# State-space mixer of a decoder trunk: order of PE's and SP's work around the scan, and a lag of 16 slots

## The reference, cut to what matters

```python
u = h @ in_w                                     # (256, 2048)
ug = u.reshape(Bsz, L, S5_GROUPS, S5_GROUP)      # 128 groups of 16 channels
bu = jnp.einsum('gnp,blgp->lbgn', b_bar, ug)     # 64 complex states a group
_, states = lax.associative_scan(combine, (a_seq, bu), axis=0)   # s[t] = lam * s[t-1] + bu[t]
y = jnp.real(jnp.einsum('gpn,lbgn->blgp', cmat, states)).reshape(Bsz, L, D)
y = y + d_skip.astype(f32) * u.astype(f32)
g = jax.nn.gelu(y).astype(h.dtype)
z = g @ glu_w + glu_b
val, gate = jnp.split(z, 2, axis=-1)
return val * jax.nn.sigmoid(gate)
```

## Time and profile before

| what | us |
|---|---|
| median of three runs | 2447.71 (2445.46 to 2448.32) |
| time of the profiled execution | 2444.28 |
| its span | 2442.5 |
| PE busy | 2392.6 (98%) |
| DVE busy | 1863.1 (76%) |
| ACT busy | 1039.8 (43%) |
| scan on DVE, first to last slot | 186.86 to 318.48 |
| first split product of the glu on PE | 338.03 |

### The profile page before, as it was taken

One profiled execution on the slowest core, in us unless ns is written; L12 is line 12 of the kernel. 1 busy time (PEld: TensorE's weight loads), 2 busy tenths in 40 slices (PEclk: granted clock), 3 DMA queues, 4 the chain that ended last, 5 costly groups with the idle time before them and its releaser, 6 DMA issues.

```text
span 2442.5 us, 34094 instructions
## 1 busy us (share of the span) xinstructions
PE 2392.6 (98%) x12953; PEld 1925.4 (79%) x12953; DVE 1863.1 (76%) x3012; ACT 1039.8 (43%) x1241; POOL 35.3 (1%) x68
## 2 busy tenths in 40 slices
PE   8999999999999999999999999999999999999998
PEld 5585578778888888888878888788888888888886
DVE  8469989878888887888879987887777754455457
ACT  5353134454434444344454434556444344434442
POOL 0000000000000000000000000000000000000000
PEclk9999999999999999999999999999999999999999
DMA  9978859779989997898758877646798666666674
GB/s 376 399 255 317 336 193 319 237 250 340 309 286 310 340 305 263 291 338 297 246 174 292 277 261 221 190 143 197 252 302 282 219 193 188 191 190 193 193 222 140
DMA packets 313338, 630.58 MB, mean 258 GB/s; under 512 B 26740, under 2 KB 27156, under 8 KB 313176
## 3 DMA queue, kind: packets, MB, share of 16 engines
q1 hardware_dynamic: 307664, 613.36, 74.7%
q0 software_dynamic: 4288, 13.90, 2.1%
q10 hardware_dynamic: 1224, 1.14, 0.1%
HBM read 626.20 MB, written 2.11 MB: 257 GB/s over the span
## 4 chain that ended last, share of the span: by engine, by line
PE 87%; DVE 9%; issue 2%; ACT 1%; DMA 0%; SPq 0%; DVEq 0%; ACTq 0%
PE psB L2288 39%; PE psA L2288 39%; DVE prod L1533 2%; DVE tmp L1538 1%; DVE st L1544 1%; PE psT L1838 1%; PE psM L1870 1%; DVE ada_acc L1209 1%; DVE w_lo L1192 1%; PE psB L2095 1%; PE psT L2288 0%; PE psT L1902 0%; PE psT L2083 0%; PE psA L2060 0%; PE psM L1850 0%
## 5 line engine op out<-in xcount | busy, mean ns | idle before, releaser
L1192 DVE TENSOR_TENSOR w_lo<-w_raw,w_hi 128x1024 fp32r<-128x1024 f32 x728 | 888.0, 1223 | 459.0 <-ACT w_hi L838 454.7
L838 ACT ACTIVATE w_hi<-w_raw 128x1024 fp32r<-128x1024 f32 x728 | 770.5, 1060 | 1095.0 <-PE psB L2288 476.3
L2288 PE MATMUL psB<-w_hi,hT_hi 128*128 128x512 f32 x1040 | 407.1, 391 | 0.0
L2288 PE MATMUL psB<-w_hi,hT_lo 128*128 128x512 f32 x1040 | 404.9, 389 | 0.0
L2288 PE MATMUL psB<-w_lo,hT_hi 128*128 128x512 f32 x1040 | 404.7, 389 | 0.0
L2288 PE MATMUL psA<-w_hi,hT_hi 128*128 128x512 f32 x1008 | 397.6, 394 | 2.3 <-DVE w_lo L1192 2.0
L2288 PE MATMUL psA<-w_hi,hT_lo 128*128 128x512 f32 x1008 | 392.9, 390 | 0.0
L2288 PE MATMUL psA<-w_lo,hT_hi 128*128 128x512 f32 x1008 | 392.4, 389 | 0.0
L1209 DVE SCALAR_TENSOR_TENSOR ada_acc<-ada_raw,csil,ada_acc 128x512 f32<-128x512 f32 x465 | 347.5, 747 | 14.6 <-DVE ada_acc L1209 0.5
L2288 PEld LDWEIGHTS psB<-w_hi,hT_hi 128*128 128x128 f32 x1040 | 195.2, 188 | 45.7 <-issue 4.5
L2288 PEld LDWEIGHTS psA<-w_hi,hT_hi 128*128 128x128 f32 x1008 | 189.2, 188 | 49.1 <-issue 8.0
(11 more groups left out here) (402 smaller groups left out, 2368.4 us busy)
## 6 DMA issues: line engine op xcount, KB each, us to landing
w_raw<-in_ffn_w_in SPq DMA_DIRECT2D x352, 512.0 KB, 4.6
ada_raw<-in_ada_w SPq DMA_DIRECT2D x496, 256.0 KB, 5.5
w_raw<-in_ffn_w_out SPq DMA_DIRECT2D x176, 512.0 KB, 4.6
col_raw<-in_ada_w SPq DMA_DIRECT2D x128, 512.0 KB, 7.4
w_raw<-in_dsa_in_w SPq DMA_DIRECT2D x112, 512.0 KB, 4.6
w_raw<-in_s_glu_w SPq DMA_DIRECT2D x56, 512.0 KB, 5.5
w_raw<-in_s_in_w SPq DMA_DIRECT2D x32, 512.0 KB, 7.9
w_raw<-in_dsa_out_w SPq DMA_DIRECT2D x32, 512.0 KB, 5.4
```

What stands on the lines that cost most here:

```text
L838: nc.scalar.activation(high(u), w_raw[:, u % RING], ACT.Copy).then_inc(w_hi_ready, 1)
L1192: V.tensor_tensor(low(u), w_raw[:, u % RING], high(u).bitcast(F32), ALU.subtract).then_inc(w_lo_ready, 1)
L2288: ins = MM(PS[s][:, t, 0:r.width] if into is None else into, a_[:, kt, tok], b_[:, kk, 0:r.width], start=kt == begin and m == 0, stop=kt = ...
```

## The change: a lag of 16 slots, and another order on PE and SP

`LEAD` becomes 16, so there are 143 slots, the second half follows 16 slots behind, and slot 16 waits for ACT's reads. On PE inputs 0 to 7 follow one another and the three pairs stand behind them; the four pairs with filler before outputs(0) are gone, and their units are spread further on: one pair behind outputs(0), as before, two among whole products 0 to 3 of token half 0, which now stand between outputs(0) and outputs(1), one behind outputs(1), and one in the inside part of piece 3. Of token half 1 whole products 0 to 2 stand before outputs(3), where there was only 0. On SP raw units 0 to 3 go ahead of column unit 46 (of 64), with the wait for all inputs; the others stay behind the column units.

```diff
@@ -66,6 +66,8 @@
 STATE_RING = 7
+FIRST_RAW = 4
+RAW_AT = FRONT + 46
 EARLY = 1
@@ -74,7 +76,7 @@
 HALF = CHUNKS // 2
-LEAD = 20
+LEAD = 16
@@ -699,14 +701,18 @@
                         elif m == 6:
                             sp.wait_ge(T_full, s5_in.turn + 3)
+                        if a == RAW_AT:
+                            sp.wait_ge(bu_full, 8)
+                            for k in range(FIRST_RAW):
+                                raw_unit(k)
                         col_unit(a)
-                    sp.wait_ge(bu_full, 8)
...
                         if whole(r, i, n // r.units):
-                            raw_unit(n)
+                            if n >= FIRST_RAW:
+                                raw_unit(n)
@@ -2133,8 +2139,7 @@
                     inputs(n)
-                    if 4 <= n < 7:
-                        units(2)
+                units(6)
@@ -2147,21 +2152,29 @@
                 for f in range(8):
                     outputs_inside(2, f)
                     units(2, 3)
-                for n in range(4):
-                    units(2, 3)
-                for half in range(2):
-                    pe.wait_ge(rec, rec_after(half, HALF - 1))
-                    for f in range(8 * half, 8 * half + 8):
-                        outputs(half, f)
-                        if f % 2:
-                            units(2)
-                    if half == 0:
+                pe.wait_ge(rec, rec_after(0, HALF - 1))
+                for f in range(8):
+                    outputs(0, f)
+                    if f % 2:
                         units(2)
+                units(2)
+                for k in range(FIRST_RAW):
+                    whole_products(k, 0)
+                    if k % 2 == 0:
+                        units(2)
+                pe.wait_ge(rec, rec_after(1, HALF - 1))
+                for f in range(8, KT):
+                    outputs(1, f)
+                    if f % 2:
+                        units(2)
+                units(2)
                 pe.wait_ge(gelu_done, 2)
                 for f in range(8, KT):
                     ins = outputs_inside(3, f)
+                    if f == 11:
+                        units(2)
                 ins.then_inc(inside_done, 1)
-                for k in range(glu.units):
+                for k in range(FIRST_RAW, glu.units):
                     whole_products(k, 0)
@@ -2170,11 +2183,12 @@
                 for f in range(8):
                     outputs(2, f)
                 early_products(glu.units - 1)
-                whole_products(0, 1).then_inc(w_used, 1)
+                for k in range(FIRST_RAW - 1):
+                    whole_products(k, 1).then_inc(w_used, 1)
                 pe.wait_ge(rec, rec_after(1, CHUNKS - 1))
                 for f in range(8, KT):
                     outputs(3, f)
-                for k in range(1, glu.units):
+                for k in range(FIRST_RAW - 1, glu.units):
                     if k == 4:
                         turn_row(2, M[:, 1], late_row)
                     whole_products(k, 1).then_inc(w_used, 1)
```

## The result

The changed kernel takes **2452.47 us** (median of 11 runs, 2450.73 to 2456.16), the kernel before, timed beside it, 2445.96 us (11 runs, 2444.44 to 2448.32). The ratio is **1.0027, 95% interval 1.002 to 1.0035**: the change costs 6.5 us. The forecast was no change (2447.9, range to 2451.3); the time lies above that range, close to the far end of the rival "the column stream makes PE late" (2452.9, which is +5.2 on the forecast's base of 2447.71).

What follows compares the result with a forecast made beforehand. PE was taken to bound the kernel (87% of the chain, DVE 9%), with PE and scan finishing almost together. +0.47 for outputs(2) starting later and -0.33 for a wait gone gave +0.1, 2447.9 us, range 2445.0 to 2451.3.

Steps and rivals of the forecast that it cites:

- the column stream makes PE late: Rival: units 46 and 47 land after 263.2, delaying PE at outputs(2); 2450.5 us, far end 2452.9; chance 0.15.
- Part 1: Scan on DVE, lag of 16 slots: 2.0 us less DVE work, but slot 16 needs the same 24 reads.
- part 2: Inputs in a row on PE cost nothing; DVE idles 3.6, slot 126 ends at 307.8, the scan at 319.4.
- part 3: Column units: eighth issued at about 200.6, not 190.6; units 46 and 47 land at 260.6, PE waits 3.1.
- third rival: PE's clock falls in idle stretches: 1.7 us for one fall, 3.4 for both, 2449.6 to 2451.3; chance 0.15.
- a granted clock under 1.00: Sign that the forecast is wrong: PE's granted clock below 1.00 between 190 and 320 us.
- Part 4: PE's order: 44.6 us of work, outputs(2) reached at 305.2, waits for slot 126 until 307.8; glu products at 338.2.
- The sum: +0.47 for the start of outputs(2), -0.33 for the wait gone: +0.1 us, forecast 2447.9.
- decisive threshold: The column stream decides once units 46 and 47 land after 263.2: 260.6 and the 2.6 PE has in hand.

Runs made afterwards that it cites:

- Number 1: The kernel before with a lag of 16 slots instead of 20 and nothing else: 2447.41 us against 2446.13, ratio 1.0004.
- number 3: The changed kernel with the three pairs of column units put back between inputs(4) and inputs(7), lag still 16: 2450.13 us against 2446.13 for before, ratio 1.0021.
- number 2: The kernel before with inputs 0 to 7 in a row and the three pairs behind them, nothing else: 2452.37 us against 2446.13, ratio 1.0025.
- number 8: The changed kernel with lag 20, pairs between inputs, raws before column unit 45, and PE's pairs and early products reordered: 2442.19 us against before's 2445.91, ratio 0.9985.
- number 10: The kernel of number 8 with the inputs in a row and six units behind them: 2450.12 us against 2446.35 for before, ratio 1.0019.
- number 11: The changed kernel with the lag of 20 slots again: 2453.14 us against 2446.35 for before, ratio 1.0029.
- number 9: The kernel of number 8 with the lag of 16 slots: 2448.26 us against 2446.35 for before, ratio 1.0006.
- number 6: The filler run: the changed kernel with 20 groups of zero matmuls in PE's long wait behind outputs(0): 2452.03 us against 2445.91 for before, ratio 1.0027.

## Why the prediction was wrong

**Part 1 (lag)** and the scan's half of **part 2** held: idle 3.46 for 3.6, slot 126 done at 308.09 for 307.8 and the scan's end at 319.69 for 319.4, both with the offset of 0.37 in them. Number 1 agrees with the price in before's order.

**The step that failed is part 3**, the column stream; its mechanism stood in the prediction, its size was off. I had units 46 and 47 land at 260.6; they were used at 265.65, 265.3 net: 4.7 late, over the 2.6 that PE had in hand. Two stretches make this up. The 19 pairs ahead of outputs(0) ended at 247.57 instead of 243.6, 3.6 net: I started the stream at its best rate, 1.285 us for a unit, but it begins at 246 to 383 GB/s. Units 6 and 7 were used at 204.83, 0.4 net behind the forecast; units 8 and 9 came 4.94 later (209.77), where I had 2 x 1.285 = 2.57, and the 28 units from there to 246.71 took 1.319 each. The 14 transfers from there (units 38 to 47 and four raws) took 18.95 us from the landing at 246.7, 1.354 each instead of 1.285: 1.0 more. The 360 GB/s of rows 6, which I had set aside because "the ring waited for PE in part", would have come near by number, but not for the right reason: from 210 on the new stream does run at 404 to 410 GB/s, but for single windows. The row that bears on it is before's own restart, 328 GB/s from 192 to 200, which I did not read. It holds POOL's `gate_bias` transfers, which the forecast left out of the stream altogether though they move with its first pair. From 204 to 210 they took 10, 27 and 8% of the DMA engines' time, 0.9 us in all, and 0.26 MB. SP's queue was also slower beside them than in the restart of number 3, which has none of them and is at its rate after some 3 us. No run moved `gate_bias`, so how much of the 3.6 is its doing is not measured.

**The clock** (third rival) came along as its consequence, not by itself. Its sign, a granted clock under 1.00, stood there twice; the fall at 212 lay ahead of waits for transfers and cost nothing. Behind the second PE was busy for all of the 47.56 us from 265.65 to 313.21 at a mean granted clock of 0.96, so an estimated 0.04 x 47.56 = 1.9 us went there. The forecast had 44.6 for this work; the last 1.1 belong to no wait, as no row of this stretch has idle time, and so are errors of my row sums. The filler run does not show that the 1.9 can be had back.

**Part 4.** With 4.7 and 3.0 PE reaches outputs(2) at 312.8 net instead of 305.2; so PE decided and not slot 126. The stretch behind it took 30.27 (forecast 30.37), outputs(3) without a wait. **The sum** was so +5.1 at the first glu product, where the forecast had +0.1; the rival's far end had +5.2. I gave that rival 0.15. The decisive threshold, 263.2, was right; the weight was not. That its 312.8 is met to the tenth is luck: it had the units land 2.9 later than they did, and the work behind them 3.0 shorter. I had put its chance by how the stream ran while it was steady, though the change itself stops it for 10 us.

**Part 2, "cost nothing",** failed as an account: that the units lie in PE's wait makes them free for PE, but each use also frees a place of the ring. Rows 3 and 4 showed the first and said nothing of the second. Part 3 did carry the 10 us of delay, but found room for them. What the row costs hangs on the order around it: 6.2 us in before's (number 2), about 8 in number 8's (number 10), and some 2.5 in the change's own (number 3), where the wait for the states stops the stream in its place.

**Not foreseen at all:** the 2.5 us in the glu stage, 2.1 of them left at the end of the span. About 1 us between these two profiled executions is chance, as said above, and some of it may lie here. Other versions have 0.6 to 2 there (0.8 in number 1, 1.1 in number 8, 0.6 in number 11). A late outputs(3) and gelu(3) are not the cause as far as number 11 tells: it has them later than the change (328.74 against 327.53 for outputs(3)) and loses only 0.6. The waits that grow are those for the low parts, the largest at the end of the stage. What makes them grow stays open; no run was made for it.

Also open: which part of the remaining loss in number 9 is the ring and which the clock, as both came with the same wait.

## What to carry to other kernels

Work that fills an engine's wait may also be what frees places of a transfer ring: before moving it, write down for each transfer when its issue becomes possible, and price the new stream from its restart, with all that the same event sets going on other queues, not at its steady rate. Where one queue feeds several consumers, its order should be the one in which they are used, and a transfer that waits for a free place should stand behind those that need none. Reordering SP and PE to that rule, with before's lag and inputs, was worth 3.7 us against before (number 8), while shortening the lag was worth nothing as long as the reads that start its second half came no sooner.

## What the runs showed of the hardware

- The stream of 512 KB transfers runs at 408 GB/s when steady. In the change it needed about 8 us from standstill to come near it (246, 383, 299, 311 GB/s in four windows of 2 us), with POOL's four transfers of 64 KB in packets under 512 bytes beside it; in number 3, with none beside it, about 3 us (from 251; 395 GB/s from 254 on).
- The landings of these transfers came 3.5 to 13.2 us after the issue in this stage of the change, where before had at most 8.3. The longest are not those of the restart (10.6 at most up to 250).
- PE's granted clock held 1.00 in a wait of 6.5 us from 259 until about 262 and was at 0.50 for the last stretch and the 2 us of full work behind it. With PE busy 0.23 of 2 us it fell behind 210 in the change (0.77, then 0.50), and stayed at 1.00 at 246 in before (rows 9). In number 6 it held 1.00 to 266 with PE busy 3.14 and 1.88 of two stretches of 4 us, and was at 0.63 in the 4 us behind, with PE busy 3.90.
- The fall can lie where the wait is cheap or where it is dear: in number 9 the clock was at 0.50 from 246 to 252, while PE worked at outputs(0) with its states already late.
